# Output projection of a decoder layer's mixer as seven block products, with block sums made by adding transfers

## The reference

```python
gates = jax.nn.sigmoid(g_logit + b_gate[l])
g_pool, g_fox = gates[..., :D], gates[..., D:]
x = x + (g_pool * y_pool + g_fox * y_fox) @ w_out[l]    # (1024 x 1024) @ (1024 x 1024)
hx = rmsnorm(x, norm_x_g[l])
mem_n = rmsnorm(mem, norm_mem_g[l])                     # 256 memory tokens, for the cross-attention
```

## Time and profile before

| | |
|---|---|
| median of 3 runs | 1446.46 us (1446.36 to 1446.65) |
| the profiled execution | 1445.97 us, of which the span of its instructions 1444.1 us |
| granted TensorE clock over the span | 0.997 |
| PE busy / DVE / ACT / POOL | 98% / 67% / 43% / 39% |
| matmuls and transposes | 7065 |
| moved by DMA | 168.45 MB, mean 117 GB/s |

### The profile page before, as it was taken

The page is one execution under the profiler, slowest core; times in us unless marked ns, Lnnn a source line. Parts: engine busy times, 40 slices in busy tenths (PEclk is TensorE's granted clock), DMA queues, the critical chain, the costliest instruction groups (busy, mean ns, idle before and its releaser), DMA issues.

```text
span 1444.1 us, 19346 instructions
## 1 busy us (share of the span) xinstructions
PE 1421.7 (98%) x7065; PEld 1171.7 (81%) x7065; DVE 974.5 (67%) x1393; ACT 619.1 (43%) x1169; POOL 558.5 (39%) x572
## 2 busy tenths in 40 slices
PE   8999999999999999999999999999999999999998
PEld 5778888887688888888888788888888888888886
DVE  7745595646877754327666887776677676785767
ACT  6545343526876642116543533332233222444445
POOL 5743233334555301005011755444444453354402
PEclk9999999999999999999999999999999999999999
DMA  8265263545333145115013213333233334883334
GB/s 212 62 116 126 52 150 76 80 101 192 112 115 102 53 161 204 59 44 147 30 44 117 73 59 110 109 110 109 83 108 110 110 110 180 304 295 96 94 103 146
DMA packets 105911, 168.45 MB, mean 117 GB/s; under 512 B 7469, under 2 KB 63297, under 8 KB 104410
## 3 DMA queue, kind: packets, MB, share of 16 engines
q1 hardware_dynamic: 99032, 147.13, 34.9%
q0 software_dynamic: 3200, 11.57, 2.2%
q10 hardware_dynamic: 3586, 8.52, 1.5%
HBM read 123.32 MB, written 42.30 MB: 115 GB/s over the span
## 4 chain that ended last, share of the span: by engine, by line
PE 91%; POOL 3%; ACT 2%; DVE 2%; issue 1%; DMA 1%; SPq 0%; DVEq 0%; ACTq 0%; POOLq 0%
PE ps L2180 28%; PE ps L2182 27%; PE ps L2181 27%; PE ps L2383 2%; PE ps L2392 2%; PE ps L2421 1%; PE ps L2422 1%; ACT prob_t L1238 1%; DMA raw_f<-in_w_in 1%; PE ps L2187 1%; ACT prob L1247 1%; PE ps L2251 1%; PE ps L2556 0%; POOL tok_f L862 0%; POOL x_t L853 0%
## 5 line engine op out<-in xcount | busy, mean ns | idle before, releaser
L2180 PE MATMUL ps<-t_lo,s_hi 128*128 128x512 f32 x308 | 119.9, 389 | 0.1
L2181 PE MATMUL ps<-t_hi,s_hi 128*128 128x512 f32 x308 | 119.8, 389 | 0.0
L2182 PE MATMUL ps<-t_hi,s_lo 128*128 128x512 f32 x308 | 119.8, 389 | 0.0
L2180 PE MATMUL ps<-h_lo_T,w_hi 128*128 128x512 f32 x256 | 100.5, 393 | 1.3 <-ACT u_t L1161 1.0
L2182 PE MATMUL ps<-h_hi_T,w_lo 128*128 128x512 f32 x256 | 99.7, 389 | 0.0
L2181 PE MATMUL ps<-h_hi_T,w_hi 128*128 128x512 f32 x256 | 99.6, 389 | 0.0
L1506 DVE TENSOR_TENSOR s_lo<-w_raw,s_hi 128x512 fp32r<-128x512 f32 x77 | 61.2, 795 | 56.8 <-ACT s_hi L1421 56.7
L1421 ACT ACTIVATE s_hi<-w_raw 128x512 fp32r<-128x512 f32 x77 | 48.7, 632 | 118.0 <-PE ps L2182 91.9
L1437 ACT ACTIVATE p_sb<-ps 128x512 f32<-128x512 f32 x22 | 13.1, 599 | 189.1 <-PE ps L2182 189.1
L2180 PE MATMUL ps<-hf_lo_T,w_hi 128*128 128x512 f32 x212 | 82.5, 389 | 0.0
L2181 PE MATMUL ps<-hf_hi_T,w_hi 128*128 128x512 f32 x212 | 82.5, 389 | 0.0
(11 more groups left out here) (378 smaller groups left out, 4310.1 us busy)
## 6 DMA issues: line engine op xcount, KB each, us to landing
w_raw<-hs_dram SPq DMA_DIRECT2D x77, 256.0 KB, 2.7
raw_p<-in_w_ffn_in SPq DMA_DIRECT2D x22, 512.0 KB, 4.6
w_raw<-in_w_ffn_in SPq DMA_DIRECT2D x22, 512.0 KB, 4.3
hs_dram<-h_sum SPq DMA_DIRECT2D x11, 1024.0 KB, 9.0
hs_dram<-hq SPq DMA_DIRECT2D x11, 768.0 KB, 7.1
wq_B<-in_w_ffn_out SPq DMA_DIRECT2D x8, 1024.0 KB, 8.0
raw_f<-in_w_in SPq DMA_DIRECT2D x14, 512.0 KB, 7.3
gate_dram<-c_st SPq DMA_DIRECT2D x28, 256.0 KB, 2.2
```

Of the source, the lines that this page charges most:

```text
L2180: nc.tensor.matmul(dst, w_h, x_l, start=start, stop=False, skip_group_check=onto)
L2181: nc.tensor.matmul(dst, w_h, x_h, start=False, stop=False, skip_group_check=onto)
L2182: return nc.tensor.matmul(dst, w_l, x_h, start=False, stop=stop, skip_group_check=onto)
```

## The change

The product z @ w_out is cut into 2 x 2 blocks of 512 x 512 and computed by seven block products instead of eight. The products are named W1 to W7, each has four steps k of 128 channels, and a step is 12 matmuls (four token tiles times `mm3`); 28 steps in all, `STEPS_W`. The order is W1, W2, W6, W4, W5, W7, W3. Products 1, 3, 5 and 7 of this order use PSUM banks 0 to 3, the others banks 4 to 7; W6, W5 and W3 add onto what the bank holds (`onto`).

- W1, W2 and W4 take blocks of z as they are; W6, W5, W7 and W3 take the block sums `z_s2`, `z_s1`, `z_s3` and `z_s4`.
- W1, W2 and W3 take the blocks `B11`, `B21` and `B22` of w_out as they are; W6, W4, W5 and W7 take the block sums `T2`, `T4`, `T1` and `T3`.
- Each of the eight sums is begun by ScalarE, which writes one addend, with its sign, as a copy of 128x2048 (`begin`, semaphore `sum_begun`), and completed by a transfer issued from POOL that adds the other addend (`accum_op=ALU.add`; `t_added` for the weight side, `s_added` for z). Each is 1 MiB. The three of T1, T3 and T2 read `w_out` in HBM, the five others read SBUF. Several chain: T2 begins from the finished T1, T4 adds the finished T2, `z_s2` begins from the finished `z_s3`, `z_s4` from the finished `z_s2`.
- `z_hi`, `z_lo` and the chunks of `w_out` in the raw buffers go. For every step ScalarE writes the high parts of 512 columns of z and 512 of weight into one slot (`step_hi`), and VectorE the low parts (`step_lo`).
- SP loads B11, B22 and B21 (3 MiB, `wo_in`) behind the gates. POOL loads `mem_in` ahead of the adding transfers.
- VectorE adds or subtracts 32 banks of 128x512 onto `xr` (`w_out_add`) instead of 16, at places of the step order given by `ADDS_AT`. The 16 transposes of `xn_m` stand behind step 17.

```diff
+W1, W2, W6, W4, W5, W7, W3 = range(7)
+W_ADDS = ([(W1, 4 + t, 0) for t in range(4)] + [(W2, 4 + t, 0) for t in range(4)] + [(W6, t, 0) for t in range(4)]
+          + [(W4, t, 0) for t in range(4)] + [(W5, t, 1) for t in range(4)] + [(W7, t, n) for t in range(4) for n in range(2)]
+          + [(W3, 4 + t, 1) for t in range(4)])
+W_FREE = {W6: 4, W4: 8, W5: 12, W7: 16, W3: 20}
+ADDS_AT = {6: (0, 1), 7: (2, 3), 10: (4, 5), 11: (6, 7), 14: (8, 9), 15: (10, 11), 18: (12, 13), 19: (14, 15), 22: (16, 17),
+           23: (18, 19), 26: (20, 21, 22, 23), 27: (24, 25, 26, 27)}
...
+            def step_hi(n):          # ScalarE
+                i, k = divmod(n, 4)
+                hi = w_hi[(C_WO + n) % SLOTS]
+                act.wait_ge(w_used, C_WO + n - SLOTS + 1)
+                if i in (W1, W2, W4):
+                    act.wait_ge(z_sum, k + 1 if i == W1 else 4 + k + 1)
+                else:
+                    act.wait_ge(s_added, {W6: 48, W5: 48, W7: 16, W3: 64}[i])
+                nc.scalar.activation(hi[:, half_of(0)], z_op(i, k), ACT.Copy)
+                if i in (W1, W2, W3):
+                    act.wait_ge(wo_in, 48)
+                else:
+                    act.wait_ge(t_added, {W6: 48, W4: 64, W5: 32, W7: 32}[i])
+                nc.scalar.activation(hi[:, half_of(1)], w_op(i, k), ACT.Copy).then_inc(hi_ready, 1)
...
+            for n in range(3, STEPS_W):
+                step_hi(n)
+                if n == 7:
+                    act.wait_ge(s_added, 48)
+                    begin(z_s4[:], z_s2[:], -1.0)
...
+            pool.wait_ge(o_lo_ready, PAIRS)
+            for t in range(2):
+                pool.dma_start(mem_in[:, t, :], mem2[tile_of(t), :]).then_inc(negc_mem_moved, 16)
+            pool.wait_ge(sum_begun, 1)
+            pool.dma_start(wo["T1"][:], wo_block(0, 1), accum_op=ALU.add).then_inc(t_added, 16)
...
+            pool.wait_ge(t_added, 48)
+            pool.dma_start(wo["T4"][:], wo["T2"][:], accum_op=ALU.add).then_inc(t_added, 16)
             pool.wait_ge(w_used, C_WO)
             for t in range(T):
                 pool.dma_start(xr[:, t, :], x2[tile_of(t), :]).then_inc(xr_loaded, 16)
+            pool.wait_ge(sum_begun, 7)
+            pool.wait_ge(z_sum, 8)
+            pool.dma_start(z_s2[:], z_all[:, 4:8, low], accum_op=ALU.add).then_inc(s_added, 16)
+            pool.dma_start(z_s1[:], z_all[:, 4:8, low], accum_op=ALU.add).then_inc(s_added, 16)
...
+            def step_lo(n):          # VectorE
+                hi, lo = w_hi[(C_WO + n) % SLOTS], w_lo[(C_WO + n) % SLOTS]
+                dve.wait_ge(hi_ready, C_WO + n + 1)
+                nc.vector.tensor_tensor(lo[:, half_of(0)], z_op(i, k), hi[:, half_of(0)].bitcast(FP32), ALU.subtract)
+                minus_hi(lo[:, half_of(1)], w_op(i, k), hi[:, half_of(1)], lo_ready)
...
+            for n in range(STEPS_W):     # TensorE
+                if k == 0:
+                    ...
+                pe.wait_ge(lo_ready, C_WO + n + 1)
+                for t in range(4):
+                    last = mm3(ps[:, 4 * (i % 2) + t, :], hi[:, tile_of(t)], lo[:, tile_of(t)], hi[:, half_of(1)], lo[:, half_of(1)],
+                               k == 0 and not onto, k == 3, onto)
+                last.then_inc(w_used, 1)
```

More of the change, by code:

```diff
@@ L320, in build @@
         o_lo = [place(f"o_lo{p}", kb + 4, [P, S], F32R) for p, kb in enumerate(o_kb)]
-        z_hi = place("z_hi", 96, [P, KD, S], F32R)
-        z_lo = place("z_lo", 128, [P, KD, S], F32R)
+        wo = {q: place(f"wo_{q}", kb, [P, 4, HALF])
+              for q, kb in {"B11": 96, "B22": 104, "B21": 112, "T1": 120, "T2": 128, "T3": 136, "T4": 144}.items()}
+        z_s1, z_s2, z_s3, z_s4 = (place(f"z_s{i}", kb, [P, 4, HALF]) for i, kb in ((1, 32), (2, 40), (3, 48), (4, 56)))
         xr = place("xr", 64, [P, T, D])
         gain = place("gain", 168, [P, D])
-        mem_in = place("mem_in", 24, [P, 2, D])
+        mem_in = place("mem_in", 152, [P, 2, D])
         xn_m = place("xn_m", 160, [P, 2, D])
@@ new lines, in begin @@
+            def begin(out, src, sign):
+                nc.scalar.activation(out, src, ACT.Copy, scale=sign).then_inc(sum_begun, 1)
+            low, high = half_of(0), half_of(1)
+            split_hi(C_FO + 3)
+            act.wait_ge(o_lo_ready, PAIRS)
+            act.wait_ge(wo_in, 48)
+            begin(wo["T1"][:], wo["B11"][:], -1.0)
+            begin(wo["T3"][:], wo["B22"][:], -1.0)
+            begin(wo["T4"][:], wo["B21"][:], -1.0)
+            step_hi(0)
+            act.wait_ge(t_added, 32)
@@ new lines, in _ @@
+            begin(wo["T2"][:], wo["T1"][:], -1.0)
+            act.wait_ge(z_sum, 4)
+            begin(z_s3[:], z_all[:, 0:4, high], -1.0)
+            step_hi(1)
+            act.wait_ge(s_added, 16)
+            begin(z_s2[:], z_s3[:], 1.0)
+            step_hi(2)
+            act.wait_ge(z_sum, 7)
+            begin(z_s1[:], z_all[:, 0:4, low], 1.0)
+            for n in range(3, STEPS_W):
[3 more added lines that the diff above has]
+                    begin(z_s4[:], z_s2[:], -1.0)
+                if n == 10:
+                    act.wait_ge(negc_mem_moved, 48)
+                    act.wait_ge(w_used, C_WO)
+                    for t in range(2):
+                        square(N_MEM + t, mem_in[:, t, :], xn_m[:, t, :])
+                if n == 20:
+                    act.wait_ge(lo_ready, C_WO + 20)
+                    for t in range(2):
+                        xt_hi_of(XT_MEM + t, 4 + 2 * t, mt_hi[:, :, tile_of(t)])
+                if n == STEPS_W - 1:
+                    for t in range(3):
+                        square_residual(t, N_CROSS, W_DONE[t], junk_x[:])
@@ L1292, in _ @@
+            for k in range(2):
+                split_hi(C_XK + k)
             for s in range(10):
@@ L1860, in _ @@
-                if k == C_WO + 7:
-                    for t in range(T):
-                        add(t, 1, T, T - 1, C_WO + 8)
+                for e in ADDS_AT.get(n, ()):
+                    w_out_add(e)
+                if n == 20:
+                    for t in range(2):
+                        xt_lo_of(XT_MEM + t, 4 + 2 * t, mt_hi[:, :, tile_of(t)], mt_lo[:, :, tile_of(t)])
+            split_lo(C_XK)
+            for e in range(28, W_ADDED):
+                w_out_add(e)
+            split_lo(C_XK + 1)
@@ L2188, in transpose_tile @@
                 last.then_inc(done, 1)
[L2190 to L2204, removed]
-                    if after:
-                        after(t)
             def front_unit_of(u):
```

174 lines of the change are left out of this document (88 added, 86 removed).

## The result

| | before | after |
|---|---|---|
| median | 1446.56 us (1446.36 to 1446.77, 4 runs) | 1465.66 us (1463.74 to 1468.48, 4 runs) |
| profiled execution, its span | 1445.97, 1444.1 | 1463.74, 1461.9 |
| mean granted clock | 0.997 | 0.991 |

The ratio is 1.0135, with a 95% interval of 1.0123 to 1.0148. The direction was forecast (slower); the time, 1465.7 us, lies above the 1452.1 forecast and just above the top of the range (1465). The profiled execution of after is the fastest of its four.

A forecast was written before the change was run, and what follows sets the result against it. TensorE, busy 98%, was taken as the bound. Matmuls -10.9, waits at steps 2, 3 and 8 +4.6, +2.7 and +7.8, small terms +1.4: +5.6 on 1446.46 gives 1452.1 us; 8-in-10 range 1438 to 1465.

The forecast's parts named there:

- The bound, and the count: TensorE bounds the kernel; in the projection 384 matmuls become 336, 48 x 0.2267 = 10.9 us less, all on the path.
- The price of an addition: Adding transfers of 1 MiB: bounded by 2.67 and 8.0 us, taken as two passes, 5.35, plus issue and signal.
- Rival C: Adding transfers much slower: three passes, or delay in POOL's making of descriptors; 1458 to 1471 us; chance 0.19.
- the estimate of 259 GB/s: Adding transfers on 16 engines, from the skill's 32.35 GB/s on two: 4.05 us each, -3.5 us, so 1443.
- The queue as the bound, steps 2, 3 and 8: New stage: TensorE waits for sums from POOL's queue, 4.6 us at step 2, 2.7 at 3, 7.8 at 8.
- `xn_x`: Before the transpose of xn_x: TensorE's 0.3 us wait goes, as the norm of tiles 0 to 2 starts earlier.
- The small waits: VectorE's order: 1.0 us lost before the transposes behind step 17, 0.7 at the first key product.
- the pace a: Price of one 1 MiB adding transfer in POOL's queue; forecast 5.0 to 6.2 us, bounds 2.67 to 8.0.
- 7a - 31.9: Change's worth in us once the queue is the bound at step 8: nothing at 4.55, +24 at 8.0.
- D: The change does not do what it says: TensorE's count stays near 7065; chance 0.01.
- A: POOL's queue before step 8: adding transfers at nearly plain pace, -8.7 to -7.1 us, 1438 to 1439; chance 0.28.

The follow-up runs named there:

- e10: e9 with additions 14 and 15 made one step earlier, behind the low part of step 18: 1437.77 us, ratio 0.9941 to before.
- e8: After, with the transfer onto T2 overwriting instead of adding (T2 lacks -T1): 1457.61 us, one run.
- e1: After, with all eight adding transfers made plain and the additions left out: 1446.70 us, ratio 1.0002 to before.
- e3: After, with begin and adding transfer of z_s3 put ahead of those of T2: 1459.42 us, ratio 1.0093 to before.
- e9: e6 with the eight block sums made by VectorE instead of GpSimd: 1438.92 us, ratio 0.9949 to before.
- e6: e5 with the square roots of the norm of tiles 0 to 2 ahead of a low part on GpSimd: 1453.80 us, ratio 1.0055 to before.
- e5: After, with no adding transfers: B12 loaded plainly, the eight block sums made by GpSimd: 1456.18 us, ratio 1.0070 to before.
- e4: After, with the two mem_in loads issued by SP instead of POOL: 1460.59 us, one run.
- e7: After, with the two plain mem_in transfers issued between the adding transfers onto T2 and z_s3: 1461.89 us, one run.

## Why the prediction was wrong

- **The bound, and the count.** Right. 48 matmuls at 0.227 us, 10.9 us less, all on the path: e10 keeps 8.4 of them.
- **The price of an addition.** The pace was right. I took two passes, 5.35 us a MiB. From 541 to 547 and 585 to 591, with only adding transfers, the engines are full at 207 and 206 GB/s, against 414 from 575 to 581, where mostly `xr` moves: 5.07 us. Rival C's three passes are refuted, as is the estimate of 259 GB/s from the Trainium skill (1443). The reason that the Trainium skill gives in "Collectives: The Full Stack", section "The bandwidth ceiling: the fold count and why AG ≠ RS ≠ AR", two reads for one write, fits: the ratio here is 2.00, the page's 1.93. My own reason does not follow from the earlier trace rows, whose one rate per window does not show reads and writes apart. The time around the pace was too small. I allowed 1 us before and 1 behind, so "about 7" for T1; it took 8.4 from issue to landing, and a plain transfer alone took 5.4 (T2 in e8) where I had 4.7.
- **The queue as the bound, steps 2, 3 and 8.** Right in place, wrong in size for step 2, and only in part right in kind. I said that the windows from 535 to 588 would show the engines full without a break. They do not: from 550 to 556 the share is 0.52, and from 549 to 552 nothing moves, since each sum waits for the landing of the one before. T3 landed at 548.7 (said 547.4), T2 was issued at 551.0, `z_s3` begun at 552.4 (said 551.2). Then the failing step: "T2 and `z_s3` move from 550.4 to 561.1, landed 562.1". That had both issued together. `z_s3` was held until T2 had landed and landed itself at 568.3, 6.2 us late: 9.7 us for 4.6. e8, where nothing holds `z_s3`, has 2.7 us in place of the 9.7 (one run, with a plain T2). Of rival C I had the right suspicion, something of fixed time in POOL's queue, in the wrong form: mainly one hold of 7 us, beside 1 to 2 us at each link of the chain.
- **The clock.** Missing from the sum. I counted a wait at its length. Behind the long ones 15 matmuls came at 0.43 us and not 0.227, 3.3 us more. The same is seen in e1 (1.6 us behind a wait of 3.2) and e3 (4.4 behind 5.7 and 7.2). It is shown beside the waits; that it comes from them rests on the granted clock, which was 1.00 in every window of the stage where no long wait was left (e9, e10). It need not fall during the wait: in e8 it stood at 1.00 through the 2.55 us before step 2 and fell behind the second matmul after it.
- **`xn_x`.** Wrong in sign: "the norm of tiles 0 to 2 starts before the end of the stage, so the 0.3 us [...] goes"; it became 2.7. I had followed ScalarE's part and not POOL's: there the square roots stand behind the low part of `w_xkv`'s third chunk, whose load waits for a raw buffer that the new order frees only at 659.3:

```profile
664.24 2.38 POOL L848 TENSOR_TENSOR w_lo<-w_raw,w_hi 128x1024 fp32r<-128x1024 f32 x1 [48.31 <-ACT w_hi L1120]
```

  The square roots start behind it, at 666.71. In before this low part starts 1.4 us behind the end of the stage, here 3.9. e6 shows it.
- **The small waits** before the transposes and at the key product: right in place, 1.3 and 1.0 for 1.0 and 0.7, since I took them as idle time and not from start to start.
- **The range.** Its ends came from one unknown, the pace a, and the additions to it (clock, hold, order on POOL) all go one way. 7a - 31.9 with the measured a of 5.07 gives +3.6. The formula had no term for what else a late queue sets off. The forecast of "slower" was right by the two-pass price, but at +3.6 that alone is hardly more than the 2.9 us that I called measurable; most of the 19.1 us came from terms that I had too small or not at all. (The 0.29 for "faster" counts D's 0.01 with A's 0.28; nothing hangs on it.)

What stays open: the rule of the hold, the 1.3 us at the start of the stage, 0.3 us of the table, and the 1.3 us from the profiled execution to the median.

## What to carry to other kernels

An addition in a transfer costs its bytes twice and has to be issued where POOL may hold it; where an engine has 2.3 us to spare for a MiB, the sum belongs there, and the choice between engines is made by who reads SBUF beside it. Count a wait of TensorE of some 3 us or more at more than its length: 1.4 to 2.6 us of lower clock came behind every wait of 3.2 to 9.6 us here, and 1.7 behind the 2.55 before step 2 in e8. Behind the waits of 2.4 to 2.7 us for `xn_x` it came in four kernels (e1, e3, e5, e8: 1.3 to 1.6 us) and not in three (after, e4, e7), so at that length the wait alone does not decide. When a stage gets shorter, follow every instruction of the next one that was hidden by its length, on every engine (here the order on POOL), and not only the stage that is changed.

## What of the hardware was not expected

- An adding transfer of 1 MiB took 8.5 us from issue to landing when alone (T2, 551.03 to 559.53) and 8.4 with another queued behind it (T1, 534.30 to 542.71). Its issue took 1.3 us of POOL, for 0.75 when it does not add (e1).
- POOL's issue of a transfer can stand still, with all that it waits for done, until an earlier adding transfer has landed: 3.0 to 7.5 us, once in each of the five kernels.
- One GpSimd operation of 4.6 to 5.1 us stretches a VectorE operation with two SBUF operands from 0.68 to 5.08 us, and leaves one with a PSUM operand at 1.22. It goes the other way too: a sum of GpSimd between VectorE's low parts took 8.01 us in e5.
